# A decoder layer on one core: lead-in steps begin with the rounded x, VectorE rounds x's second half, convolution operations move to rounds 8 to 10

## The chip, the cores and the metric

The kernel runs on one core of one Trainium2 chip. Its time is the device time of one execution in microseconds (us). The engines are TensorE (PE, with its weight loads as PEld), VectorE (DVE), ScalarE (ACT), GpSimd (POOL) and SyncE (SP), which here only issues transfers. Line numbers are those of the kernel before unless said otherwise.

## The reference

One decoder layer over x (1024 tokens of 1024 features, float32), cut to what matters:

```python
shift, scale, gate = jnp.split(silu(c) @ w_ada + b_ada, 3, axis=-1)
h = _rms_norm(x, norm_w) * (1.0 + scale) + shift
q, k, v, gate_a, u, gate_b = jnp.split(h @ w_in, splits, axis=-1)
q, k = rope(rms_norm(q)), rope(rms_norm(k))
y_a = sliding_window_sink_attention(q, k, v, sinks) * silu(gate_a)
y_b = conformer_conv(u, ...) * silu(gate_b)   # GLU, 31 causal taps, LayerNorm, SiLU
x = x + gate * (jnp.concatenate([y_a, y_b], -1) @ w_out)
```

## The kernel before

**Products of matrices.** Each float32 factor is split into a part rounded to float32r ("hi") and the rest ("lo"). A product is three matmuls: hi by hi, lo weight by hi x, hi weight by lo x. `channel_step` issues these three for one 128-row block k of the 1024 features; eight blocks make a channel tile (128 output channels by 512 tokens). `h[:, 0]` holds the rounded modulated x, `h[:, 1]` its rest.

**The lead-in.** x is transposed by TensorE (`x_transposes(idx)`, idx 0 to 7 for the first 512 tokens, 8 to 15 for the second) into the two banks of `tr`. ScalarE's `modulate(idx)` reads a bank twice: it writes the modulated x unrounded (`h32`, two buffers) and then rounded (`h[:, 0]`), and then counts `a_h32`. VectorE's `split_h(idx)` subtracts the two (`h[:, 1]`) and counts `d_hlo`. For the modulation of block k a column of adaLN is needed: VectorE sums it (`ada_sums`, slabs of `w_ada` by eight transfers' worth of rows), TensorE adds it over the partitions (`ada_cols(k)`), ScalarE turns it into `modA`, `modB` (`factors`). In lead-in step k TensorE runs block k of four channel tiles at once (`early`), after waiting for `d_hlo`. `keep_busy` issues matmuls whose result is not used.

**After the lead-in.** Channel tile 4 runs from the first 512 tokens; tile 5 does too, with the transposes of x's second half between its steps; tile 6 is the first that reads the second half, and waits at each block for `d_hlo`. Tiles 7 to 15 follow. ScalarE and VectorE make the GLU from them (`tanh_g`, `glu`), which frees the banks. VectorE also adds up the gate columns (`gate_sum(0..7)`, each from a 512 KB transfer into the ring `raw` of three buffers, which the weights share: a buffer is loaded again when its sum counts `d_gp`).

**The convolution** is 200 VectorE operations in a fixed list (`conv_order`); `conv(n)` issues the next n. They stand between other work of VectorE: 62 before the rounds, the rest in the rounds.

**The rounds** n = 0 to 15. In round n TensorE projects Q, K, V of token block n (n under 8, `L777` to `L779`) or a gate channel tile, and between the steps runs attention: `transpose_qk` and `scores` of block n - 2, `transpose_p` and `times_v` of block n - 4. VectorE in its round n does the RoPE of block n - 1, `previous_keys` and `row_max` of block n - 2, `denominators` of n - 3, gates (`gate`, from n = 8) and convolution operations. The order on each engine is the order of the code; engines meet only through semaphores.

**LayerNorm of the convolution.** After the last operation VectorE adds the four channel blocks (`channel_sum`), TensorE adds over the partitions (`ln_mean`, L796, then `ln_var`, L804), VectorE copies the variance out, GpSimd makes the reciprocal deviations (L517), and `ln_scale` (L812) spreads that row over the partitions into `ps`; `normed` and `swish` of VectorE wait for it.

The lines at the places named:

```python
for dst in (h32[:, idx % 2, :], h[:, 0, k, half * HALF:(half + 1) * HALF]):   # L955, ScalarE
pe.wait_ge(d_hlo, k + 1)                                                     # L601, lead-in step
gate_sum(0); gate_sum(1); gate_sum(2)                                        # L1290, VectorE
if (m, half, k) == (6, 1, 6): ln_scale()                                     # L829, TensorE
```

## Time and profile before

| | us |
|---|---|
| median of 3 runs (430.77 to 432.27) | 431.35 |
| the profiled execution, its own time | 431.71 |
| its span | 430.0 |
| PE busy | 408.4 (95%) |
| DVE busy | 334.0 (78%) |
| ACT busy | 217.5 (51%) |
| POOL busy | 110.0 (26%) |

The span runs from the first to the last instruction; 1.71 us of the execution lie around it. Matmuls are pipelined and their ends modelled, so PE's busy time says when it had work, not that it ran at its peak. An idle time in brackets behind a row names what ended it.

### The profile page before, as it was taken

To read this page: it belongs to the slowest core of one execution; us is meant where nothing else is said; L and a number is where in the kernel's file an instruction comes from. 1 tells how busy PE (TensorE), PEld (TensorE's weight loads), DVE (VectorE), ACT (ScalarE), POOL (GpSimd) and SP (SyncE) were. 2 spreads that over 40 slices of the span, in tenths; PEclk is the share of its full clock that TensorE was granted. 3 is DMA by queue.
4 is the path that set the end of the run, shared out by engine and by line. 5 is a ranking of instruction groups with operands and counts; after the bars stand their busy time and mean duration, and the time that the engine had idled before them with its cause. 6 is when DMAs were issued, how large, how long until landed. Compare 5 with 4: busy or idle time off the path is not lost.

```text
span 430.0 us, 5914 instructions
## 1 busy us (share of the span) xinstructions
PE 408.4 (95%) x2102; PEld 327.6 (76%) x2102; DVE 334.0 (78%) x554; ACT 217.5 (51%) x496; POOL 110.0 (26%) x150
## 2 busy tenths in 40 slices
PE   0899998999999998999999999999999999999996
PEld 0577785888888887778776767777788888888886
DVE  2789777599999999999989797799995996222222
ACT  3768777025211137887788989524166784100000
POOL 1400050002420443354225316973031005100000
PEclk9999998999999999999999999999999999999999
DMA  7999656306930000004003466993637059951111
GB/s 274 353 316 351 243 178 207 99 0 167 231 61 2 6 8 7 7 2 155 0 8 91 75 124 124 166 103 71 125 74 124 2 195 252 259 125 49 50 49 50
DMA packets 54327, 51.40 MB, mean 120 GB/s; under 512 B 19271, under 2 KB 49275, under 8 KB 54298
## 3 DMA queue, kind: packets, MB, share of 16 engines
q1 hardware_dynamic: 38256, 41.50, 31.0%
q0 software_dynamic: 15904, 9.44, 16.8%
q8 instruction: 17, 0.28, 0.3%
q10 hardware_dynamic: 138, 0.09, 0.1%
q14 instruction: 12, 0.10, 0.1%
HBM read 46.82 MB, written 4.19 MB: 119 GB/s over the span
## 4 chain that ended last, share of the span: by engine, by line
PE 54%; DVE 28%; issue 3%; ACT 2%; DMA 1%; POOL 1%; DVEq 0%; ACTq 0%
PE pm L573 7%; PE pm L574 6%; PE pm L575 6%; DVE cacc L1326 4%; PE pm L846 4%; PE pm L845 4%; PE pm L847 4%; DVE cacc L1346 3%; DVE z L1333 3%; PE tr L846 3%; PE tr L845 3%; PE tr L847 3%; PE ps L702 2%; DVE cacc L1333 2%; DVE z L1346 2%
## 5 line engine op out<-in xcount | busy, mean ns | idle before, releaser
L573 PE MATMUL pm<-h,wts 128*128 128x512 f32 x224 | 90.4, 404 | 1.3 <-DVE gb L1461 0.8
L574 PE MATMUL pm<-h,wts 128*128 128x512 f32 x224 | 87.6, 391 | 0.0
L575 PE MATMUL pm<-h,wts 128*128 128x512 f32 x224 | 87.4, 390 | 0.0
L573 PEld LDWEIGHTS pm<-h,wts 128*128 128x128 f32 x224 | 42.2, 188 | 13.4 <-issue 2.4
L575 PEld LDWEIGHTS pm<-h,wts 128*128 128x128 f32 x224 | 42.2, 188 | 9.1
L574 PEld LDWEIGHTS pm<-h,wts 128*128 128x128 f32 x224 | 42.3, 189 | 8.2 <-issue 0.2
L921 ACT ACTIVATE wts<-raw 128x1024 fp32r<-128x1024 f32 x30 | 31.2, 1051 | 33.4 <-PE pm L575 17.4
L777 PE MATMUL pm<-wts,h 128*128 128x256 f32 (+1 forms) x128 | 45.1, 352 | 0.1
L778 PE MATMUL pm<-wts,h 128*128 128x256 f32 (+1 forms) x128 | 43.1, 337 | 0.0
L779 PE MATMUL pm<-wts,h 128*128 128x256 f32 (+1 forms) x128 | 43.1, 337 | 0.0
L440 POOL DMA_DIRECT2D wts<-in_w_in x22 | 28.8, 2697 | 51.6 <-ACT wts L923 51.6
L1333 DVE SCALAR_TENSOR_TENSOR z<-z,cw 128x513 f32<-128x513 f32 x42 | 31.7, 754 | 3.8 <-POOL pcur L483 3.6
L1053 ACT ACTIVATE sel<-sel,nmx,rsq 128x128 f32<-128x128 f32 x64 | 30.7, 482 | 2.2 <-DVE sdiff L1445 2.0
L440 POOL DMA_DIRECT2D wts<-in_w_out x12 | 13.4, 1275 | 68.0 <-ACT wts L923 68.0
L777 PEld LDWEIGHTS pm<-wts,h 128*128 128x128 f32 x128 | 24.2, 189 | 6.7 <-issue 3.5
L845 PE MATMUL pm<-wts,h 128*128 128x512 f32 x72 | 28.0, 389 | 0.0
L846 PE MATMUL pm<-wts,h 128*128 128x512 f32 x72 | 28.0, 389 | 0.0
L847 PE MATMUL pm<-wts,h 128*128 128x512 f32 x72 | 28.0, 389 | 0.0
L1617 DVE TENSOR_TENSOR obuf<-pm,gbc 128x512 f32<-128x512 f32 x9 | 6.2, 692 | 27.4 <-PE pm L847 27.4
L956 ACT ACTIVATE h<-tr,modB,modA 128x512 f32<-128x512 f32 (+1 forms) x32 | 22.8, 777 | 7.0 <-PE tr L537 4.8
L779 PEld LDWEIGHTS pm<-wts,h 128*128 128x128 f32 x128 | 24.2, 189 | 2.7
L778 PEld LDWEIGHTS pm<-wts,h 128*128 128x128 f32 x128 | 24.3, 190 | 2.3
(209 smaller groups left out, 901.7 us busy)
## 6 DMA issues: line engine op xcount, KB each, us to landing
slab<-in_w_ada SPq DMA_DIRECT2D x16, 512.0 KB, 8.2
raw<-in_w_in SPq DMA_DIRECT2D x14, 512.0 KB, 4.9
xs<-in_x SPq DMA_DIRECT2D x8, 512.0 KB, 8.8
raw<-in_w_ada SPq DMA_DIRECT2D x8, 512.0 KB, 4.5
xr<-in_x SPq DMA_DIRECT2D x8, 512.0 KB, 5.9
out<-xr SPq DMA_DIRECT2D x15, 256.0 KB, 2.7
wts<-in_w_in POOLq DMA_DIRECT2D x6, 512.0 KB, 9.5
raw<-in_w_in SPq DMA_DIRECT2D x8, 256.0 KB, 8.0
```

The source lines that it names most:

```text
L440: gp.dma_start(to, src, accum_op=ALU.add).then_inc(g_add[ADDED.index(i)], 16)
L573: pe.matmul(out, hi_w, hi_x, start=first, stop=False)
L574: pe.matmul(out, lo_w, hi_x, start=False, stop=False)
L575: return pe.matmul(out, hi_w, lo_x, start=False, stop=last)
L777: pe.matmul(o, x_hi, w_hi, start=(k == 0), stop=False)
L778: pe.matmul(o, x_hi, w_lo, start=False, stop=False)
L779: last = pe.matmul(o, x_lo, w_hi, start=False, stop=(k == KT - 1))
L845: pe.matmul(o, h[:, 0, k, ts], w[0], start=(k == 0), stop=False)
L846: pe.matmul(o, h[:, 0, k, ts], w[1], start=False, stop=False)
L847: return pe.matmul(o, h[:, 1, k, ts], w[0], start=False, stop=(k == KT - 1))
L921: act.activation(whalf(i, 0), src, ACT.Copy).then_inc(a_hi, 1)
L1333: ins = dve.scalar_tensor_tensor(out=tmp, in0=src, scalar=weight, in1=tmp, op0=ALU.mult, op1=ALU.add)
```

## The change

- `a_hr` is a new semaphore. In the first half of x, ScalarE writes the rounded x first and counts `a_hr`, then writes `h32` and counts `a_h32`.
- A lead-in step waits for `a_hr` and runs the eight matmuls that read the rounded x (both weight parts, four tiles), then waits for `d_hlo` and runs the four that read the rest. `ada_cols(k + 1)` stands between the second and the third tile of the eight. The four `keep_busy` matmuls of step 2 are gone; of those after `ada_cols(1)`, one and a half banks stand before the transposes and none behind them (before: two and one and a half).
- Channel tile 4 has its 16 matmuls with the rounded weights first, waiting for ScalarE's `a_hi`; the 8 with the weights' rest follow after `wait_split`.
- In the second half of x ScalarE writes `h32` alone; VectorE copies it to `h[:, 0]`, waits for that copy, and subtracts.
- VectorE's order: `gate_sum(0)`, the eight split steps, the first two `glu`, then `gate_sum(1)` to `(7)` (before: sums 0 to 2, split steps with sums 3 to 5 between, sums 6 and 7, and the two `glu` later).
- Convolution operations: 18 become 16 before the rounds; in round 0 11 become 5, in round 1 4 become 3, in round 9 9 become 8, in round 10 9 become 12, in round 11 12 become 11; rounds 8 and 9 get 4 more each behind `row_max`. The list and its length of 200 stay.
- `ln_scale` is issued three steps sooner, in front of step 3 of tile (6, 1) and not of step 6.

```diff
             keep_busy(pm[:, 2, :], 2)
             ada_cols(1)
-            keep_busy(pm[:, 2, :], 2)
+            keep_busy(pm[:, 2, :], 1)
+            keep_busy(pm[:, 2, 0:256], 1)
             x_transposes(0)
             x_transposes(1)
-            keep_busy(pm[:, 2, :], 1)
-            keep_busy(pm[:, 2, 0:256], 1)
...
                 if 0 < k < KT - 1:
                     x_transposes(k + 1)
-                    if k == 2:
-                        pe.wait_ge(a_ab, 4)
-                        keep_busy(ps[:, 1, 256:512], 4)
-                    if k > 1:
-                        ada_cols(k + 1)
-                pe.wait_ge(d_hlo, k + 1)
+                pe.wait_ge(a_hr, k + 1)
                 if k % 2 == 0:
                     pe.wait_ge(d_wlo, k // 2 + 1)
                 for e, (bank, slot, col) in enumerate(early):
-                    if (k, e) == (1, 3):
-                        ada_cols(2)
-                    last = channel_step(bank, slot, col, 0, k)
+                    if e == 2 and 0 < k < KT - 1:
+                        ada_cols(k + 1)
+                    for part in range(2):
+                        pe.matmul(bank, wts[:, slot + 1, part, k, col:col + P], h[:, 0, k, 0:HALF],
+                                  start=(k == 0 and part == 0), stop=False)
+                pe.wait_ge(d_hlo, k + 1)
+                for bank, slot, col in early:
+                    last = pe.matmul(bank, wts[:, slot + 1, 0, k, col:col + P], h[:, 1, k, 0:HALF],
+                                     start=False, stop=(k == KT - 1))
...
             pe.wait_ge(a_ab, 16)
+            pe.wait_ge(a_hi, 6)
+            for k in range(KT):
+                for part in range(2):
+                    pe.matmul(ps[:, 1, :], wts[:, 3, 0, k, 0:P], h[:, part, k, 0:HALF], start=(k == 0 and part == 0), stop=False)
             wait_split(pe, 2)
-            channel_tile(4, ps[:, 1, :], 2, 0, 0)
+            for k in range(KT):
+                last = pe.matmul(ps[:, 1, :], wts[:, 3, 1, k, 0:P], h[:, 0, k, 0:HALF], start=False, stop=(k == KT - 1))
+            last.then_inc(p_main, 1)
...
-                        if (m, half, k) == (6, 1, 6):
+                        if (m, half, k) == (6, 1, 3):
                             ln_scale()
...
-                for dst in (h32[:, idx % 2, :], h[:, 0, k, half * HALF:(half + 1) * HALF]):
-                    last = act.activation(dst, tr[:, idx % 2, :], ACT.Identity, scale=modA[:, k:k + 1],
-                                          bias=modB[:, k:k + 1])
-                last.then_inc(a_h32, 1)
+                if idx < KT:
+                    act.activation(h[:, 0, k, half * HALF:(half + 1) * HALF], tr[:, idx % 2, :], ACT.Identity,
+                                   scale=modA[:, k:k + 1], bias=modB[:, k:k + 1]).then_inc(a_hr, 1)
+                act.activation(h32[:, idx % 2, :], tr[:, idx % 2, :], ACT.Identity, scale=modA[:, k:k + 1],
+                               bias=modB[:, k:k + 1]).then_inc(a_h32, 1)
...
                 dve.wait_ge(a_h32, idx + 1)
+                if idx >= KT:
+                    link(dve.tensor_copy(h[:, 0, k, sl], h32[:, idx % 2, :]))
...
-            gate_sum(0)
-            gate_sum(1)
-            gate_sum(2)
-            for idx in range(KT, 2 * KT):
-                split_h(idx)
-                if idx < KT + 3:
-                    gate_sum(idx - KT + 3)
-            gate_sum(6)
-            gate_sum(7)
...
+            gate_sum(0)
+            for idx in range(KT, 2 * KT):
+                split_h(idx)
+            glu(0, 0, pm[:, 2, :], 2, 1)
+            glu(1, 0, ps[:, 0, :], 3, 2)
+            for i in range(1, KT):
+                gate_sum(i)
...
                 if n == 0:
-                    conv(11)
+                    conv(5)
```

The order of VectorE's instructions behind the normalised x of the second half (`xs`), before; `h<-h_64,h` is the subtraction, `gacc` a gate sum, `z` the GLU, `h_64` the buffers `h32`:

```order
L1223 TENSOR_SCALAR xs<-xs,rsx 128x1024 x4
L1283 TENSOR_SCALAR gacc<-raw,cact 128x1024
L1286 SCALAR_TENSOR_TENSOR gacc<-raw,cact,gacc 128x1024 x2
L1246 TENSOR_TENSOR h<-h_64,h 128x512
L1286 SCALAR_TENSOR_TENSOR gacc<-raw,cact,gacc 128x1024
...
L1246 TENSOR_TENSOR h<-h_64,h 128x512 x5
L1286 SCALAR_TENSOR_TENSOR gacc<-raw,cact,gacc 128x1024 x2
```

And the same place now (its line numbers are those of the changed kernel); the pair of `CAST` and subtraction stands there eight times:

```order
L1230 TENSOR_SCALAR xs<-xs,rsx 128x1024 x4
L1292 TENSOR_SCALAR gacc<-raw,cact 128x1024
L1254 CAST h<-h_64 128x512
L1255 TENSOR_TENSOR h<-h_64,h 128x512
...
L1303 SCALAR_TENSOR_TENSOR z<-z,pm 128x2x256
L1303 SCALAR_TENSOR_TENSOR z<-z,ps 128x2x256
L1295 SCALAR_TENSOR_TENSOR gacc<-raw,cact,gacc 128x1024 x7
```

Seven gate sums moved behind the last split step and the first two GLU operations; eight copies came in.

TensorE in lead-in step 2, before: the transposes of block 3 (`tr`), the unused matmuls, the adaLN column, then twelve matmuls in threes per tile:

```order
L537 MATMUL tr<-ident,xs 128x128 x4
L546 MATMUL ps<-ones 128x256 x4
L567 MATMUL ps<-ones,ada_acc 128x1 x2
L573 MATMUL pm<-h,wts 128x512
L574 MATMUL pm<-h,wts 128x512
L575 MATMUL pm<-h,wts 128x512
```

And now, where L602 reads the rounded x and L606 the rest:

```order
L537 MATMUL tr<-ident,xs 128x128 x4
L602 MATMUL pm<-h,wts 128x512 x4
L567 MATMUL ps<-ones,ada_acc 128x1 x2
L602 MATMUL pm<-h,wts 128x512 x2
L602 MATMUL ps<-h,wts 128x512 x2
L606 MATMUL pm<-h,wts 128x512 x3
L606 MATMUL ps<-h,wts 128x512
```

The adaLN column moved behind four matmuls that do not need it, and the matmuls with x's rest moved to the step's end.

VectorE at the end of round 8, before: the row maxima of block 6 (`nmx`), then the gates of rounds 8 and 9:

```order
L1439 TENSOR_REDUCE nmx<-sel_51 128x8
L1442 TENSOR_TENSOR nmx<-nmx,rsq 128x8
L1444 TENSOR_TENSOR nmx<-nmx,nsnk 128x8
L1445 TENSOR_TENSOR sdiff<-nmx,snk 128x8
L1461 SCALAR_TENSOR_TENSOR gb<-gb,pm 128x512 x2
```

And now:

```order
L1444 TENSOR_REDUCE nmx<-sel_51 128x8
L1447 TENSOR_TENSOR nmx<-nmx,rsq 128x8
L1449 TENSOR_TENSOR nmx<-nmx,nsnk 128x8
L1450 TENSOR_TENSOR sdiff<-nmx,snk 128x8
L1333 SCALAR_TENSOR_TENSOR z<-z,cw 128x512
L1353 SCALAR_TENSOR_TENSOR cacc<-z,cws,cacc 128x512
L1343 SCALAR_TENSOR_TENSOR z<-z,cols 128x512
L1349 TENSOR_TENSOR z<-z 128x527
L1466 SCALAR_TENSOR_TENSOR gb<-gb,pm 128x512 x2
```

Four convolution operations moved in front of the two gates.

## Rows read from the trace of the kernel before

**Rows 1.** The page, part 1: busy us (share of the span) x instructions.

```profile
PE 408.4 (95%) x2102; PEld 327.6 (76%) x2102; DVE 334.0 (78%) x554; ACT 217.5 (51%) x496; POOL 110.0 (26%) x150
```

**Rows 2.** Timeline, PE, lead-in: start, duration, instructions merged [idle before <- what ended it].

```profile
17.05 2.74 PE L546 MATMUL pm<-ones 128*128 128x512 f32 x4
19.63 1.04 PE L537 MATMUL tr<-ident,xs 128*128 128x128 f32 x8
...
22.50 0.50 PE L573 MATMUL pm<-h,wts 128*128 128x512 f32 x1 [0.54 <-DVE h L1246]
...
30.03 1.89 PE L546 MATMUL ps<-ones 128*128 128x256 f32 x8
...
47.53 0.58 PE L567 MATMUL ps<-ones,ada_acc 128*128 128x1 f32 x4 [0.39 <-DVE ada_acc L1239]
...
53.85 0.39 PE L573 MATMUL ps<-h,wts 128*128 128x512 f32 x1
```

**Rows 3.** Timeline, ACT and DVE, lead-in.

```profile
20.27 1.45 ACT L956 ACTIVATE h<-tr,modB,modA 128x512 f32<-128x512 f32 x2 [1.94 <-PE tr L537]
...
23.88 0.69 DVE L1246 TENSOR_TENSOR h<-h,h 128x512 fp32r<-128x512 f32 x1 [0.65 <-ACT h L956]
...
31.05 0.69 DVE L1246 TENSOR_TENSOR h<-h,h 128x512 fp32r<-128x512 f32 x1 [0.46 <-ACT h L956]
...
44.47 2.46 DVE L1235 SCALAR_TENSOR_TENSOR ada_acc<-slab,cact,ada_acc 128x256 f32<-128x256 f32 x6
```

**Rows 4.** Timeline, PE, tiles 5 (`pv`), 6 and 7 (`pm`).

```profile
69.56 0.90 PE L537 MATMUL tr<-ident,xs 128*128 128x128 f32 x4 [1.34 <-ACT h L956]
...
72.25 0.78 PE L573 MATMUL pm<-h,wts 128*128 128x512 f32 x1
...
78.26 0.39 PE L573 MATMUL pm<-h,wts 128*128 128x512 f32 x1
78.94 0.39 PE L573 MATMUL pm<-h,wts 128*128 128x512 f32 x1
```

**Rows 5.** Windows: stretch, then busy us of PE, PEld, DVE, ACT, POOL; granted clock.

```profile
71.00:72.00 1.00, 1.00 (x5) 0.60 (x5) 0.66 (x1) 1.00 (x3) 0.00 (x0) 0.50 0.77 259
...
240.00:260.00 20.00, 20.00 (x112) 15.17 (x111) 17.78 (x30) 18.45 (x45) 5.82 (x8) 1.00 0.63 113
260.00:280.00 20.00, 20.00 (x113) 14.92 (x112) 14.65 (x26) 15.08 (x42) 18.42 (x24) 1.00 1.00 154
```

**Rows 6.** Timeline, DVE, gate sums to the first convolution operations.

```profile
58.38 0.75 DVE L1223 TENSOR_SCALAR xs<-xs,rsx 128x1024 f32<-128x1024 f32 x1 [0.71 <-POOL rsx L434]
...
74.72 2.67 DVE L1286 SCALAR_TENSOR_TENSOR gacc<-raw,cact,gacc 128x1024 f32<-128x1024 f32 x2
...
84.70 0.49 DVE L1323 TENSOR_SCALAR cacc<-z,cw 128x512 f32<-128x512 f32 x1
...
97.43 2.35 DVE L1252 TENSOR_TENSOR wts<-raw,wts 128x1024 fp32r<-128x1024 f32 x2
```

**Rows 7.** The page, part 6: KB each, median us from issue to landing.

```profile
raw<-in_w_ada SPq DMA_DIRECT2D x8, 512.0 KB, 4.5
```

**Rows 8.** Timeline, DVE and PE, weights' rest of unit K0 and round 3.

```profile
130.27 2.35 DVE L1252 TENSOR_TENSOR wts<-raw,wts 128x1024 fp32r<-128x1024 f32 x2
...
134.51 0.28 PE L777 MATMUL pm<-wts,h 128*128 128x256 f32 x1
...
166.67 1.13 PE L702 MATMUL ps<-kT,qT 64*128 64x256 f32 x8 [1.58 <-DVE sel L1427]
```

**Rows 9.** Timeline, DVE, PE and POOL, row of means to row of deviations.

```profile
306.64 1.23 DVE L1476 TENSOR_TENSOR lnA<-lnA,z 128x1024 f32<-128x1024 f32 x1
...
307.92 1.98 PE L796 MATMUL ps<-lnA,ones 128*128 128x512 f32 x4
...
321.44 1.67 POOL L517 TENSOR_TENSOR rsx<-tiny,mhalf 128x8 f32<-128x8 f32 x1
...
325.10 1.95 PE L812 MATMUL ps<-ident,rsx 128*128 128x128 f32 x16
```

More of the change, by code:

```diff
@@ L1307, in glu @@
                                          op0=ALU.add, op1=ALU.mult).then_inc(d_glu, 1)
+            gate_sum(0)
[5 more added lines that the diff above has]
+                gate_sum(i)
+            dve.memset(z[:, :, :].rearrange("p c (b m) -> p c b m", b=2)[:, :, :, 0:PAD // 2], 0.0).then_inc(d_link, 1)
+            linked[0] += 1
             done = [0]
@@ L1357, in _ @@
             pads = linked[0]
-            glu(0, 0, pm[:, 2, :], 2, 1)
-            glu(1, 0, ps[:, 0, :], 3, 2)
             glu(0, 1, pm[:, 1, :], 7, 5)
@@ L1365, in _ @@
             glu(1, 1, ps[:, 0, :], 9, 6)
-            conv(18)
+            conv(16)
             glu(2, 0, pm[:, 2, :], 12, 3)
@@ L1517, in _ @@
                 if n == 9:
-                    conv(9)
+                    conv(8)
                 if n == 10:
@@ L1526, in _ @@
                 if n == 10:
-                    conv(9)
+                    conv(12)
                 if n == 11:
-                    conv(12)
+                    conv(11)
                     channel_sum(1)
@@ L1543, in _ @@
                     row_max(b2)
-                if n == 1:
-                    conv(4)
+                if n in (1, 8, 9):
+                    conv({1: 3, 8: 4, 9: 4}[n])
                 if 8 <= n < 15 and n != 10:
```

4 lines of the change are left out of this document (1 added, 3 removed).

## The prediction

> **What bounds the kernel now.** I read the page's part 1 first: PE is busy for 408.4 of 430.0 us, DVE for 334.0 [rows 1]. So the time can fall only where PE idles, runs at its lower clock, or issues matmuls that nobody needs; those 21.6 idle us had to be found by the timeline of PE. It shows four places. Before 22.50 PE waits for the first modulated x. In the lead-in it waits 0.39 for a column of adaLN in step 6, and step 2 carries four unused matmuls, from 30.03 to 31.76 [rows 2]. In the second half of x it waits for ScalarE, the longest 1.34, and then works at clock 0.50, the lower of its two levels (1.2 GHz and not 2.4) [rows 4, 5]. In round 3 it waits 1.58 for VectorE [rows 8]. The chain of waits adds the second fact: from 84 to 184 us it runs on VectorE almost alone, through the convolution. PE hardly idles there, so the two engines are level. A gain of PE in the lead-in is kept only if VectorE comes sooner by as much; otherwise it turns into new waits of PE.
>
> **1. The first half of x.** PE's steps. The transposes start at 19.63, behind two unused banks of which the first runs at the low clock; half a bank fewer stands there now. VectorE's x is ready just then, so I put the start at 19.2. ScalarE took the first bank 0.64 after the start of the transposes, and its two writes last 1.45 together, 0.75 each [rows 2, 3]. With the rounded x first, PE can start 0.64 + 0.75 + 0.1 behind 19.2, at 20.7, where it started at 22.50: 1.8 sooner.
>
> What follows is set by VectorE. Its work in a lead-in step is the split (0.60 to the next start), six sums (2.46) and the last add (0.35): 3.4, and 4.6 where it also makes the weights' rest (1.15); PE's own is 12 matmuls x 0.227, the transposes 0.43, the column 0.36: 3.5. From 31.05 to 47 VectorE has no pause, so the lead-in moves by what its pauses give before that: 0.65 at 23.88 and 0.46 at 31.05, both waits for ScalarE's second write [rows 3]. ScalarE's first step is 0.5 sooner, and its step 2 follows a column that PE now reaches 2.3 sooner; of the 1.11 I take 0.95. So the last column is ready at 46.4 where it was at 47.35. Then PE: column until 46.75, eight matmuls of step 6 until 48.6, while ScalarE makes the factors and the last rounded x (0.6 + 0.75, ready at 48.25), step 7 with 12 matmuls until 51.35. Tile 4 began at 53.85 [rows 2]: **2.5 sooner**. More than VectorE's 0.95, since behind the last column nothing waits for the unrounded x and its split any longer, and two thirds of a step are left to fill the time. The four unused matmuls cost nothing then and give nothing now: VectorE's pace hides them. PE has new pauses instead, at the columns: by the same sums 1.0, 0.5, 1.1 and 0.95 us. Tile 4's new order is free: ScalarE's last weights are there at 50.8, VectorE's rest at 52.2, and 16 matmuls run from 51.35 to 55.0.
>
> **2. The second half.** Before, tile 4 starts at 53.85 and tile 6 ends at 78.26, 24.4 us [rows 2, 4]. PE's own work there is 3 tiles x 8 blocks x 0.68 (row 78.94 less row 78.26) and eight transposes x 0.44: 19.85. So 4.55 are waits and low clock. After: x's last block is normalised at 59.05, behind ScalarE's squares [rows 6], which start 1.2 sooner: 57.9, where PE would want it at 57.5; 0.35 of waiting stays. Then ScalarE has one write of 0.75 per block, not two, and no gate sum (1.28) stands between VectorE's splits. VectorE's block is a copy and a subtraction. The copy is in no row; the nearest above is the subtraction, 0.69 with the same output, the nearest below a tensor_scalar of 512 elements, 0.49 [rows 3, 6]. I take the lower, since it also has one source; the pair then is 0.45 + 0.05 + 0.65, about 1.2, and 1.5 by the upper end. Eight pairs from 59.4 end at 69.0 (71.4 by the upper end). PE wants the last at 71.0, so even the upper end costs 0.4. Tile 6 ends at 71.7: **4.05 sooner, 6.55 in all**.
>
> On such a copy the Trainium skill ("VectorE: DVE Perf Modes", section "Mode 2×_2P — use both read ports for one tensor") says that an op with one tensor from SBUF reads it through both ports and gives two results a cycle even in float32, which an op with two tensors cannot. By that rule the sum is the one above, by 0.69 it is 0.4 less of a gain; the two rows agree with the rule, but no row here shows it for an output in float32r.
>
> **3. What VectorE owes for it.** The gate sums 1 to 7 now stand behind the splits and two glu (69.0 + 1.2 = 70.2). Three find their data in the ring. The fourth is issued when sum 1 frees its buffer (71.5), and a transfer lands after 4.5, 3.5 at best [rows 7]; with 1.28 per sum (2.67 for two [rows 6]) the four late ones end at 76.9, 78.2, 79.7 and 81.7 (81.0 at best, 83.5 if each waits its 4.5). The convolution starts at 82.6 (81.9 to 84.4), before at 84.70: **2.1 sooner**, not 6.5. From here the due times, VectorE against PE:
> - 20 operations take 12.7 (84.70 to 97.43), 0.66 each [rows 6]. The weights' rest for tile 12 is ready at 97.6; PE, 6.5 sooner, wants it at 99. Free.
> - 18 to 16 operations give 1.3 more. K0's first rest was ready at 131.4 and is at 128.0; PE wanted it at 134.51 and wants it at 128.0 [rows 8]. I price 0.1; each us that the convolution starts later than 82.6 costs a us here.
> - Round 0 loses six operations (4.0) and round 1 one (0.66): VectorE is 3.4 + 4.65 = 8.1 sooner from round 2.
> - Round 3: PE comes 6.5 sooner, VectorE 8.1, so the 1.58 shrinks to nothing and PE is 8.0 sooner. From round 4 the chain of waits was PE's and stays PE's.
> - The operations taken out (2 + 6 + 1) come back: 4 in round 8, 4 - 1 in round 9, 3 in round 10, less 1 in round 11, nine net, up to ten ahead at once, 6.6 us. VectorE's idle time there was 2.22 + 5.35 = 7.57 [rows 5]. They fit if they fall where it waited; not all will. Row maxima and probabilities of the last blocks may come up to 1 us late, and I charge 0.5.
>
> **4. The deviations' row.** PE issues it at 325.10, and GpSimd had it ready at 323.11. Three steps sooner is 3 x 0.68: 323.06 [rows 9]. So PE waits 0.05 and a semaphore's time, 0.2 by my estimate, and the normed blocks start 1.8 sooner. PE never waited for those, so I book **0.2 lost**. Bounds: 0 to 1.
>
> **The sum**: -6.55 + 0.1 - 1.5 (round 3) + 0.5 + 0.2 = -7.25, rounded up to -7.5 for small waits of PE in rounds 5 to 12 which an earlier VectorE ends. The profiled execution took 431.71, 0.36 over the median of 431.35. From it 424.2, from the median 423.85; I say **424.0**.
>
> **Rivals.**
> *A. VectorE keeps the middle.* If nine operations in rounds 8 to 11 find no idle time (ScalarE's tanh waits in turn for VectorE), VectorE reaches the row of means only by its earlier start. There both are level: its last sum ends at 307.87, PE's row starts at 307.92 [rows 9]. Gain then 2.1 plus about half of 2.6: 428.5. For: the chain; against: 7.57 us idle.
> *B. The clock falls in the lead-in.* Before, it fell after the pause of 1.34, and cost half of the some 3.8 us spent at 0.50 [rows 4, 5]. The new pauses at the columns are up to 1.1. Each fall costs up to 1.9, of which VectorE's pace hides a part: with two, 426.8. Before, PE was without a pause of 0.4 in these steps thanks also to the four unused matmuls. The Trainium skill ("TensorE: Matmul & The Clock Gate", section "What's actually happening") speaks against the change here: the clock is set by how busy TensorE has been of late, so taking away unused work can lower it. By that rule the time would be this rival's; the rows show one fall after long pauses and none after 0.39 or 0.54.
> *C. More.* If rounds 8 to 11 cost nothing and small waits go: 422.0.
> *D. Slower: the splits hold everything.* If copy, subtraction and ScalarE's write run one after another (0.75 + 0.69 + 0.61 and three semaphore times of 0.1: 2.35 per block), eight blocks from 59.4 end at 78.2, and the convolution starts at 89.3, 4.6 later than before; K0's rest then holds PE by 1.2 beyond its old time, and with VectorE's waits in rounds 8 to 11 only half filled the row of means comes 2.5 later: 434. It decides from 84.70 on: a convolution that starts later loses. Against: two `h32` buffers and two banks let the write run beside the split.
> *E. The change does not do what it says.* If the adaLN transfers, and not VectorE, pace the lead-in and PE's transposes pace the second half, nothing moves before 70 us: 430.8.
>
> **Chances.** Forecast 0.56 (422.6 to 425.8), A 0.14, B 0.13, C 0.07, D 0.06, E 0.04. The range from 422.0 to 428.8 holds the forecast, B and the better part of A and C. What this measurement tells from no change is 0.3%, 1.3 us. Faster: forecast, A, B, C, 0.90; the same: E, 0.04; slower: D, 0.06.
>
> **What would show it.** In the changed profile: PE's first projection matmul at 20.7; tile 4 at 51.4; the `CAST` at 0.49 or below, and the last subtraction near 69; tile 6 ending at 71.7 with granted clock 1.00 from 65 to 75; the gate sums ending near 81.7, with two waits for `raw`; the first convolution operation at 82.6; no wait above 0.5 at K0's weights; no wait of PE for `sel` in round 3; VectorE's idle time from 232 to 272 under 2.5; the row of means at 300; the row of deviations 0.2 late. I am wrong if the convolution starts after 84.7, if the clock in the lead-in is under 1.00, or if PE waits for VectorE before the row of means by more than 1 us.

## The result, and the profile after

The changed kernel takes 427.74 us (median of 5 executions, 427.46 to 428.81); the kernel before, measured beside it, 431.80 (430.77 to 432.27). The ratio is 0.9916 (95% interval 0.9898 to 0.9934): 3.6 us faster by the ratio, 4.06 by the medians. 424.0 us were forecast, 7.4 sooner than the 431.35 from which the forecast started. So the direction was right and half of the gain was missing. The same two kernels measured once more, further below, gave 0.9910 (0.9897 to 0.9922).

The profiled execution of the changed kernel has a span of 426.2 us against 430.0. The page's part 1, which answers to [rows 1]:

```profile
PE 402.5 (94%) x2090; PEld 323.7 (76%) x2090; DVE 337.7 (79%) x562; ACT 212.4 (50%) x488; POOL 113.4 (27%) x150
```

VectorE has eight operations more and ScalarE eight fewer, the copies; TensorE has 12 matmuls fewer.

**The lead-in.** Timeline of PE; the columns are start, duration, instruction, and in brackets the idle time before it and what ended it. It answers to [rows 2].

```profile
21.22 1.66 PE L602 MATMUL pm<-h,wts 128*128 128x512 f32 x6 [0.43 <-ACT h L962]
...
47.38 0.58 PE L567 MATMUL ps<-ones,ada_acc 128*128 128x1 f32 x4 [0.94 <-DVE ada_acc L1246]
...
52.48 0.84 PE L627 MATMUL ps<-h,wts 128*128 128x512 f32 x3
```

The first projection matmul comes 1.3 us sooner, the new pauses at the columns are there (0.94 before the last), and tile 4 starts at 52.48 where it was at 53.85. In twelve further traces that share this lead-in and keep the clock, tile 4 starts between 51.59 and 52.22; this execution is 0.3 to 0.9 later than they are.

**The second half and the gate sums.** Timeline of VectorE (`L1254` is the copy, `L1255` the subtraction, `L1295` the gate sums), which answers to [rows 6]:

```profile
68.67 0.43 DVE L1254 CAST h<-h 128x512 fp32r<-128x512 f32 x1
69.13 0.69 DVE L1255 TENSOR_TENSOR h<-h,h 128x512 fp32r<-128x512 f32 x1
...
75.75 1.29 DVE L1295 SCALAR_TENSOR_TENSOR gacc<-raw,cact,gacc 128x1024 f32<-128x1024 f32 x1 [0.74 <-DMA raw<-in_w_ada]
78.08 1.28 DVE L1295 SCALAR_TENSOR_TENSOR gacc<-raw,cact,gacc 128x1024 f32<-128x1024 f32 x1 [1.04 <-DMA raw<-in_w_ada]
80.11 2.67 DVE L1295 SCALAR_TENSOR_TENSOR gacc<-raw,cact,gacc 128x1024 f32<-128x1024 f32 x2 [0.75 <-DMA raw<-in_w_ada]
...
83.98 0.49 DVE L1330 TENSOR_SCALAR cacc<-z,cw 128x512 f32<-128x512 f32 x1
```

The copy is 0.43 us and the last subtraction starts at 69.13, as forecast. TensorE has no low clock here any more, and tile 7 starts at 73.12 where it started at 78.26 [rows 4]:

```profile
73.12 0.39 PE L573 MATMUL pm<-h,wts 128*128 128x512 f32 x1
```

```profile
65.00:75.00 10.00, 10.00 (x52) 8.38 (x51) 9.64 (x14) 3.67 (x6) 0.00 (x0) 1.00 0.16 47
```

That row is a window: stretch, its length, busy time of PE, PEld, DVE, ACT, POOL, granted clock. So 5.1 us of the lead are in hand. But three gate sums wait for their rows, 2.5 us together, and the convolution starts only 0.7 sooner. What holds its start has changed: before, VectorE had its gate sums done and stood still for TensorE's tile 7 right in front of it,

```profile
83.90 0.69 DVE L1306 SCALAR_TENSOR_TENSOR z<-z,pm 128x512 f32<-128x512 f32 x1 [4.83 <-PE pm L575]
```

and now the gate sums themselves end at 82.78, after tile 7.

**The stretch in which it was decided.** I cut both traces at two events: VectorE's first convolution operation, and TensorE's row of means, which follows VectorE's last channel sum. One window of the kernel before:

```profile
84.70:307.92 223.22, 219.90 (x1220) 174.64 (x1218) 211.03 (x352) 125.73 (x346) 86.13 (x112) 1.00 0.40 74
```

and of the changed kernel, with the two windows that answer to [rows 5]:

```profile
83.98:304.03 220.05, 215.41 (x1201) 171.03 (x1199) 211.06 (x352) 125.78 (x346) 88.95 (x112) 1.00 0.41 78
240.00:260.00 20.00, 18.98 (x104) 13.90 (x104) 19.14 (x32) 18.06 (x54) 8.61 (x13) 1.00 0.67 129
260.00:280.00 20.00, 17.84 (x98) 12.93 (x95) 17.16 (x29) 11.51 (x28) 19.86 (x22) 1.00 0.98 124
```

The reader should look at the DVE column: 352 operations and 211.0 us in both. The stretch is VectorE's load plus its pauses: 211.03 + 12.19 before, 211.06 + 8.99 after. The gain at the row of means is therefore 0.72 (start of the convolution) + 3.20 (pauses) - 0.03 = 3.89, and from there to the end of the span the two take 122.0 and 122.2. Such a sum could be written for any engine. That VectorE is the right one shows at the stretch's end: the row of means starts 0.06 us behind VectorE's last sum,

```profile
302.75 1.22 DVE L1481 TENSOR_TENSOR lnA<-lnA,z 128x1024 f32<-128x1024 f32 x1
304.03 1.98 PE L802 MATMUL ps<-lnA,ones 128*128 128x512 f32 x4
```

and 0.05 to 0.09 behind it in all 17 traces of this case, although the row lies anywhere from 300.02 to 308.15. So nothing that TensorE gains in between counts by itself. The waits of VectorE in this stretch (us in total, times, longest), before:

```profile
DVE gb L1461 <- ACT gb L1103: 3.9, 5, 1.4
DVE z L1333 <- POOL pcur L483: 3.6, 2, 2.9
DVE wts L1252 <- ACT wts L921: 1.1, 1, 1.1
```

and after:

```profile
DVE z L1353 <- POOL pcur L483: 3.4, 2, 2.8
DVE wts L1261 <- ACT wts L927: 1.1, 1, 1.1
DVE nmx L1444 <- POOL sel L504: 1.0, 1, 1.0
```

The waits at the gates, 3.9 us, are filled by the moved operations. The waits for GpSimd's masks of the probabilities (`pcur`) are not: 3.6 before, 3.4 after. One for GpSimd's part of the scores (`sel`) is new; it ends at 151.89, long before rounds 8 to 11. `L1353` waits by the kernel's own code: in rounds 10 and 11 VectorE stops for `g_mask` before more convolution operations.

**The masks.** GpSimd's timeline, blocks 6 and 7, before (each mask is L477, L481, L483):

```profile
261.24 0.63 POOL L477 TENSOR_SCALAR_AFFINE_SELECT pprev<-pcur 128x512 f32<-128x512 f32 x1 [12.06 <-ACT pcur L1035]
...
274.52 0.63 POOL L477 TENSOR_SCALAR_AFFINE_SELECT pprev<-pcur 128x512 f32<-128x512 f32 x1
```

and after:

```profile
255.36 1.08 POOL L477 TENSOR_SCALAR_AFFINE_SELECT pprev<-pcur 128x512 f32<-128x512 f32 x1 [11.18 <-ACT pcur L1042]
...
269.45 2.88 POOL L477 TENSOR_SCALAR_AFFINE_SELECT pprev<-pcur 128x512 f32<-128x512 f32 x1
```

The same instruction takes 2.88 where it took 0.63. It starts at 269.45, 5.07 sooner than before, beside the ninth of VectorE's run of twelve operations, and ends at 272.33, 0.5 behind that run's last:

```profile
271.09 0.74 DVE L1340 SCALAR_TENSOR_TENSOR z<-z,cw 128x513 f32<-128x513 f32 x1
274.64 0.75 DVE L1353 SCALAR_TENSOR_TENSOR z<-z,cws 128x512 f32<-128x512 f32 x1 [2.81 <-POOL pcur L483]
```

**The deviations' row.** GpSimd has the deviations ready at 319.22, and TensorE's row follows at 319.27, where it stood 2.0 us behind them before [rows 9]; VectorE's wait for the row fell from 3.8 to 2.0:

```profile
317.55 1.67 POOL L517 TENSOR_TENSOR rsx<-tiny,mhalf 128x8 f32<-128x8 f32 x1
```

### The profile page after: what moved, and what is told of

Read it like the earlier page. It is cut to its first block, busy times and chain, and to the rows that moved or that the text cites. A ratio compares the mean times of both kernels' runs of the same rounds, so it can differ in the third digit from the quotient of the medians.

```text
span 426.2 us, 5891 instructions
## 1 busy us (share of the span) xinstructions
PE 402.5 (94%) x2090; PEld 323.7 (76%) x2090; DVE 337.7 (79%) x562; ACT 212.4 (50%) x488; POOL 113.4 (27%) x150
## 4 chain that ended last, share of the span: by engine, by line
PE 52%; DVE 23%; POOL 6%; ACT 3%; issue 3%; DMA 1%; DVEq 0%; ACTq 0%; POOLq 0%
PE pm L783 4%; PE pm L573 4%; PE pm L784 4%; PE pm L785 4%; PE pm L575 4%; PE pm L574 4%; PE pm L852 4%; PE pm L851 4%; PE pm L853 4%; DVE cacc L1333 3%; PE tr L852 3%; PE tr L851 3%; PE tr L853 3%; POOL wts L440 2%; PE ps L708 2%
## 5 line engine op out<-in xcount | busy, mean ns | idle before, releaser
L573 PE MATMUL pm<-h,wts 128*128 128x512 f32 x200 | 79.8, 399 | 0.8 <-DVE gb L1466 0.8
L575 PE MATMUL pm<-h,wts 128*128 128x512 f32 x200 | 77.9, 390 | 0.0
L574 PE MATMUL pm<-h,wts 128*128 128x512 f32 x200 | 77.9, 390 | 0.0
L573 PEld LDWEIGHTS pm<-h,wts 128*128 128x128 f32 x200 | 37.5, 188 | 11.1 <-issue 2.4
L575 PEld LDWEIGHTS pm<-h,wts 128*128 128x128 f32 x200 | 37.5, 188 | 8.0
L574 PEld LDWEIGHTS pm<-h,wts 128*128 128x128 f32 x200 | 37.6, 188 | 7.5 <-issue 0.2
L1353 DVE SCALAR_TENSOR_TENSOR z<-z,cws 128x512 f32<-128x512 f32 x30 | 22.4, 748 | 3.8 <-POOL pcur L483 3.4
```

The lines of the kernel that those rows point to most:

```text
L573: pe.matmul(out, hi_w, hi_x, start=first, stop=False)
L574: pe.matmul(out, lo_w, hi_x, start=False, stop=False)
L575: return pe.matmul(out, hi_w, lo_x, start=False, stop=last)
```

## The experiments

Theory T1: GpSimd's masks are held up while VectorE's convolution operations run without a gap, and that is what the moved operations cost. Theory T5: VectorE's load and its pauses set the row of means. The rivals stand in the expectations. All ratios are against the kernel before, measured beside each kernel (its median there was 431.25 to 431.80); so ratios compare better than medians. "Stretch" is first convolution operation to row of means, as above, in one profiled execution of each kernel. "Small masks" leaves out most of the last three blocks' masks and does not compute the layer.

| kernel | convolution starts | stretch | row of means | median us | ratio (95% interval) |
|---|---|---|---|---|---|
| before | 84.70 | 223.2 | 307.92 | 431.80 | 1 |
| changed | 83.98 | 220.05 | 304.03 | 427.74 | 0.9916 (0.9898 to 0.9934) |
| counts back | 82.71 | 223.2 | 305.92 | 430.61 | 0.9985 (0.9972 to 0.9997) |
| counts alone | 84.05 | 224.1 | 308.15 | 431.92 | 1.0021 (1.0006 to 1.0036) |
| lead-in alone | 83.71 | 223.3 | 307.02 | 430.57 | 0.9980 (0.9966 to 0.9994) |
| ScalarE writes both | 85.18 | 220.4 | 305.55 | 429.59 | 0.9959 (0.9943 to 0.9974) |
| fewer at round 10 | 82.76 | 220.9 | 303.63 | 428.01 | 0.9934 (0.9914 to 0.9954) |
| no stop for the masks | 83.55 | 224.2 | 307.71 | 431.77 | 1.0001 (0.9986 to 1.0016) |
| small masks | 82.91 | 217.1 | 300.02 | 424.60 | 0.9842 (0.9826 to 0.9858) |

**1. The counts back.** One of the six counts:

```diff
                 if n == 0:
-                    conv(5)
+                    conv(11)
```

> The changed kernel with the convolution's operations spread over the rounds as in the kernel before (18 for 16 ahead of the rounds, 11 for 5 in round 0, 4 for 3 in round 1, 9 and nothing extra in rounds 8 and 9, then 9 and 12); everything else of the change stays. Theory T1 (contention: GpSimd's masks are slowed by VectorE operations put beside them in rounds 8 to 10): with fewer operations beside them the masks of blocks 5 and 6 need 0.63, 0.42 and 0.41 us each again and the L477 of block 7 falls from 2.88 us to about 0.63; but eight operations more (8 x 0.67 = 5.3 us) stand ahead of round 0, where the convolution starts only 0.7 us sooner than before, so that the first matrix product of the rounds waits on VectorE again and the rounds start 4 to 5 us later than in the changed kernel: 429.5 to 431 us. Rival R3 (the second half and lead-in gain is simply lost later, whatever VectorE does): 427.7 us, as the changed kernel.

Measured 430.61 us: T1's range. L477 is 0.63 again in blocks 6 and 7 (0.62 in the trace of block 6):

```profile
259.20 0.62 POOL L477 TENSOR_SCALAR_AFFINE_SELECT pprev<-pcur 128x512 f32<-128x512 f32 x1 [12.06 <-ACT pcur L1042]
...
272.50 0.63 POOL L477 TENSOR_SCALAR_AFFINE_SELECT pprev<-pcur 128x512 f32<-128x512 f32 x1
```

The rest of the change without the counts shortens nothing behind 82.71: the stretch is 223.2, to 0.01 that of before. But the range does not speak for T1 alone. The first product of the rounds waits 3.0 us for VectorE, as the expectation also said, and TensorE's clock is 0.58 from 142 to 146 behind it. And VectorE waits for the masks as long as before the change, though nothing holds them up:

```profile
DVE z L1340 <- POOL pcur L483: 3.6, 2, 2.9
```

So the masks' waits are there without any hold-up, and the second half of T1, that the hold-up is what the moved operations cost, is not shown.

**2. Fewer at round 10.**

```diff
-                    conv(12)
+                    conv(8)
...
-                    conv(11)
+                    conv(15)
```

> The changed kernel with 8 instead of 12 operations of the convolution in round 10 and 15 instead of 11 in round 11, after the masks of block 7; all else as changed. T1 (contention): VectorE's run of back-to-back operations ends at 269.1 instead of 271.8 us, L477 of block 7 (starts 269.45) takes 0.6 to 0.9 us instead of 2.88, the masks end at 271 to 271.5 instead of 274.56, VectorE waits for them about 2 us and the PV product of block 7 does not wait 1.39 us; four more operations then stand ahead of the first channel sum: it starts 0.5 to 1.0 us sooner (286.41 before the edit), total 426.7 to 427.2 us. Rival R2 (GpSimd is slow there by itself, as the tail of its eight DMA issues of 10.35 us that come just before): L477 keeps 2.9 us, the masks end at 274.6, and the four operations come on top: first channel sum 2.7 us later, 430 us.

```profile
268.25 1.03 POOL L477 TENSOR_SCALAR_AFFINE_SELECT pprev<-pcur 128x512 f32<-128x512 f32 x1
```

L477 falls to 1.03 and with it R2 (GpSimd is slow there by itself), since the eight DMA issues of 10.35 us stand in front of it as before. But no time came of it (428.01): the stretch is 0.8 longer, where I expected 0.5 to 1.0 less. VectorE now waits 3.59 for the masks instead of 2.81, and the four operations still have to be done. T1's mechanism held, my price of it did not: VectorE's twelve operations were useful work, and what counts is how long it stands still for the masks. With four of them behind the masks these end at 271.56 and not at 274.61, and nothing is gained by it.

**3. The counts alone**: the kernel before, with the six edits of the first experiment the other way, as

```diff
                 if n == 10:
-                    conv(9)
+                    conv(12)
```

> The kernel before with the change's counts of convolution operations alone (16, 5, 3, 8, 12, 11 and 4 more in rounds 8 and 9), nothing else of the change. The rounds start 2.5 to 3 us sooner, as the waits of TensorE for VectorE at the first product of the rounds (1.58 us) and round 3 go; T1: in rounds 8 to 11 the masks cost 2.5 to 3 us more as in the changed kernel, so that 0 to 1.5 us of it are left: 430 to 431.8 us. Rival R3 (the loss in rounds 8 to 11 comes with the earlier second half, not with the operations moved there): the full 2.5 to 3 us stay, 428.5 to 429.2 us.

431.92 us, 0.2% slower than before and 0.1 us above T1's range. The masks of block 7 are held up just as much (2.88), so it is the counts and not the earlier start that do it. L477 shows how the lead goes: it starts 2.1 us sooner than before in block 5, 1.8 in block 6, 0.95 in block 7, and the row of means comes 0.2 later. VectorE, now early, waits for TensorE's products instead:

```profile
DVE ssq L1386 <- ACT v L1029: 3.6, 2, 3.3
DVE z L1346 <- POOL pcur L483: 3.3, 2, 2.8
```

Together with experiment 1: neither the counts nor the rest of the change shortens the stretch (+0.9 and 0.0), both together do by 3.2. By the ratios the counts alone lose 0.9 us, the rest alone gains 0.6, both together gain 3.6.

**4. The second gate sum ahead of the splits.**

```diff
             gate_sum(0)
+            gate_sum(1)
             for idx in range(KT, 2 * KT):
```

> The changed kernel with the second gate sum in front of the eight splits of the second half, not behind them (as before three stood there). Theory T4: the gate sums are bound by the landing of their rows (waits of 0.74, 1.04 and 0.75 us behind the splits), since each sum frees the buffer for a later load; with one more in front, a load starts 6 us sooner and one of the three waits goes, the convolution starts 0.7 us sooner, the splits start 0.7 us later but have waits for the transposes of x to take that: 427.0 to 427.7 us. Rival: the loads are slow by themselves and all waits stay, and the second half's products start 0.7 us later: 427.7 to 428.4 us.

426.86 us, ratio 0.9903 (0.9889 to 0.9917), a little under both ranges. The convolution starts at 81.53, but the waits for rows are still 0.69, 1.34 and 0.50, as long as before the edit. The stretch grows to 220.7. See 12.

**5. No stop for the masks.**

```diff
                 if n == 11:
-                    dve.wait_ge(g_mask, 2 * NT)
                     conv(5)
```

> The changed kernel without VectorE's wait for the masks of block 7 in round 11 (it stood ahead of five operations of the convolution and one gate, and took 2.81 us in the trace of the changed kernel). T1 (VectorE's operations hold up GpSimd's masks as long as they run without a gap): VectorE goes on, L477 of block 7 (starts 269.45) and the five masks behind it take until VectorE comes to its next gap or wait, so they end at 276 to 278 instead of 274.56 us; TensorE's PV product of block 7 waits 3 to 5 us instead of 1.39; VectorE's first channel sum comes up to 2.8 us sooner; in all 427 to 429 us. Rival R2 (the 2.88 us are GpSimd's own): masks still end at 274.6, VectorE gains its 2.81 us, 425.2 us.

```profile
268.82 6.21 POOL L477 TENSOR_SCALAR_AFFINE_SELECT pprev<-pcur 128x512 f32<-128x512 f32 x1
275.10 0.41 POOL L481 TENSOR_SCALAR_AFFINE_SELECT pcur<-pcur 128x256 f32<-128x256 f32 x1
```

```profile
273.78 0.75 DVE L1333 SCALAR_TENSOR_TENSOR z<-z,cw 128x512 f32<-128x512 f32 x1
```

```profile
277.36 1.12 PE L739 MATMUL pv<-pcur,vmix 128*64 128x256 f32 x4 [4.73 <-POOL pcur L483]
```

This is the clearest showing of T1. An instruction that takes 0.63 takes 6.21 and ends 0.5 behind VectorE's last operation; the next one, with VectorE still, takes its 0.41. Rival R2 falls. The total (431.77, all of the change's gain lost) was worse than I wrote: VectorE's first channel sum comes 3.7 us later and not sooner, since VectorE then waits 7.11 us for ScalarE's part of a gate, and TensorE's clock is 0.56 in a stretch that holds its own wait:

```profile
274.00:280.00 6.00, 2.64 (x16) 1.07 (x16) 0.53 (x1) 0.00 (x0) 5.86 (x10) 0.56 0.20 26
```

**6. The third gate sum ahead, too.**

```diff
             gate_sum(0)
+            gate_sum(1)
+            gate_sum(2)
             for idx in range(KT, 2 * KT):
```

> As the experiment with the second gate sum ahead of the splits, with the third there too. T4 (a gate sum behind the splits is bound by its row's landing, each early sum starts one load sooner): VectorE waits for no row behind the splits or for one, the convolution starts another 0.7 us sooner, the splits start 0.7 us later: 426 to 427 us. Rival: two sums ahead already use up the slack ahead of the splits, the second half of the products of x starts 0.7 us later and the rounds with it: 427 to 427.7 us.

427.5 us. The convolution starts at 81.38, no sooner than with two sums (0.7 was expected), and tile 6 starts 0.9 later; the stretch is 222.0, with 1.7 us of new waits of VectorE for TensorE's products. The rival was right.

**7. ScalarE writes both** (no copy on VectorE).

```diff
-                if idx < KT:
+                if True:
                     act.activation(h[:, 0, k, half * HALF:(half + 1) * HALF], ...)
...
-                if idx >= KT:
-                    link(dve.tensor_copy(h[:, 0, k, sl], h32[:, idx % 2, :]))
```

> The changed kernel with ScalarE writing both h and h32 in the second half again, VectorE not copying. Theory (ScalarE's two ACTIVATEs of a step set the pace of the second half before, and the copy took that away): the eight steps are 0.3 to 0.5 us longer each, tile 7 starts 3 to 4 us later (near 76.5 us) and VectorE's splits end as much later, but it saves VectorE 8 x 0.43 = 3.4 us; the rounds start 0.5 to 3 us later: 428.5 to 430 us. Rival (VectorE's total is what counts up to the rounds): unchanged or sooner, 426.5 to 427.7 us.

429.59 us, within the theory's range. VectorE's subtractions then wait 0.65 each for ScalarE, every 1.34 us instead of 1.13, and tile 6 starts at 68.35 against 66.6 to 67.6. In the kernel with the lead-in alone, which has the gate sums between the splits as well, it starts at 71.71. So of the second half's gain the copy brings 1 to 2 us and the gate sums' new place about 3 (3.4, less the 0.5 by which that kernel's tile 4 starts later).

**8. The lead-in alone**: the kernel before, with the change's `modulate` order for all 16 steps and TensorE's part up to tile 4.

```diff
-                for dst in (h32[:, idx % 2, :], h[:, 0, k, half * HALF:(half + 1) * HALF]):
+                if True:
+                    act.activation(h[:, 0, k, half * HALF:(half + 1) * HALF], ...).then_inc(a_hr, 1)
+                act.activation(h32[:, idx % 2, :], ...).then_inc(a_h32, 1)
```

> The kernel before with the lead-in part alone (in all sixteen steps ScalarE writes the rounded x first, TensorE's products of the rounded x come ahead of those of the rest, the extra products that keep TensorE busy in step 2 are gone, tile 4 in the order of the change). By the trace of the changed kernel the first half ends 2.0 us sooner, net of the start; the second half is still ScalarE's pace: it starts 2 us sooner and all of it stays up to the gate sums, where rows that land late take 0.5 to 1 us back: 429.8 to 430.6 us. Rival (the lead-in's gain ends at the gate sums' rows): 431.2 us, as before.

430.57 us: 0.2% faster, as expected. Tile 4 starts at 52.22, the convolution at 83.71.

**9. Small masks.**

```diff
+                if b >= 5:
+                    gp.affine_select(out=pprev[g][0:64, :, 0:8], in_=pcur[g][0:64, :, 0:8], ...)
+                    gp.affine_select(out=pcur[g][0:64, :, 0:8], in_=pcur[g][0:64, :, 0:8], ...)
+                    return
```

> The changed kernel with GpSimd's masks of blocks 5, 6 and 7 cut to a corner of 64 x 8 elements a head in two operations instead of three full ones (the rest of these masks is left out, so the attention of the last blocks is not the reference's). Theory T5 (from conv start to the mean row VectorE is the bound: 211.0 us of work plus its waits, 9.0 us, of which 3.4 are for these masks): both waits for the masks nearly go (0.5 to 1 us left), TensorE's 0.83 and 1.39 us before the PV products go, the row of the means comes 2.4 to 3 us sooner, 424.8 to 425.5 us. Rival T6 (TensorE is the bound in rounds 9 to 11, VectorE's waits are slack): it gains at most TensorE's 2.2 us of waits or less, 426 us or more.

The masks are cut to a corner here and the result is not the layer's; the run only prices them. 424.60 us, 3.1 below the changed kernel's median, slightly more than expected. The stretch falls from 220.05 to 217.11:

```profile
82.91:300.02 217.11, 215.28 (x1201) 171.05 (x1200) 209.83 (x352) 125.87 (x346) 83.09 (x106) 1.00 0.42 80
```

VectorE's same 352 operations are 1.2 us shorter, its pauses 1.7. T5 holds and T6 falls. What the run prices is all of the masks' work, the waits for them and VectorE's slower operations beside them, and not the hold-up alone. Even a mask of 64 x 32 elements is held:

```profile
267.27 1.75 POOL L477 TENSOR_SCALAR_AFFINE_SELECT pprev<-pcur 64x32 f32<-64x32 f32 x1 [1.10 <-ACT pcur L1050]
269.09 0.23 POOL L481 TENSOR_SCALAR_AFFINE_SELECT pcur<-pcur 64x32 f32<-64x32 f32 x1
```

**10. The unused matmuls back in step 2.**

```diff
+                    if k == 2:
+                        pe.wait_ge(a_ab, 4)
+                        keep_busy(ps[:, 1, 256:512], 4)
                 pe.wait_ge(a_hr, k + 1)
```

> The changed kernel with the four extra products of step 2 (256 columns each) that keep TensorE busy in the lead-in. The granted clock is 1.00 in the lead-in without them, so they only cost their own time where TensorE does not wait, 4 x 0.11 to 0.2 us: 427.7 to 428.3 us. Rival (the clock is only just held without them, so that some executions lose it): median 427.4 us or less.

```profile
29.68 1.89 PE L546 MATMUL ps<-ones 128*128 128x256 f32 x8
31.22 1.28 PE L605 MATMUL pm<-h,wts 128*128 128x512 f32 x4
```

428.75 us, ratio 0.9937 (0.9924 to 0.9949), 1.0 above the changed kernel: they take 1.54 of TensorE's time, tile 4 starts at 53.36, the convolution at 84.74. That is above both expectations; the lead-in is TensorE's at that point and nothing hides them. The six executions lie within 0.5 us (428.43 to 428.90), those of the changed kernel within 3.0.

**11. The deviations' row back; small operations in the waits.**

```diff
-                        if (m, half, k) == (6, 1, 3):
+                        if (m, half, k) == (6, 1, 6):
                             ln_scale()
```

> The changed kernel with the deviations' row back at step 6 of that product, from step 3. The end after the mean row was as long before and after (122.1 us each from the mean row to the end of the span), although VectorE's wait for the row fell from 3.8 to 2.0 us. Theory (that wait is slack): 427.7 us, within 0.2. Rival (it carried 0.5 us or more, hidden by another loss): 428.2 to 429 us.

427.08 us, ratio 0.9904 (0.9888 to 0.9919), below both ranges, but the intervals of the two kernels overlap. The traces are sharper. The row of means to the end of the span takes 121.98 to 122.04 us in the five traces that have the row at step 6 (this one, the kernel before, the counts alone, the lead-in alone and the last kernel of experiment 12), and 122.22 to 122.27 in the twelve that have it at step 3. The sooner row costs 0.2 us, although VectorE's wait for it is 1.8 shorter.

```diff
             gate_sum(0)
             gate_sum(1)
...
-            for i in range(2, KT):
+            for i in range(2, 5):
                 gate_sum(i)
+            (the memset of z's padding, lnc, cws)
+            for i in range(5, KT):
+                gate_sum(i)
```

> The experiment with the second gate sum ahead of the splits (426.86 us), and VectorE's memset of the padding and its small operations on the columns (0.16, 0.32 and 0.21 us) moved from behind the gate sums to behind the fifth, where VectorE waits for a row. Theory T5 (each us by which VectorE's convolution starts sooner comes off the end, since VectorE is the bound up to the mean row): the convolution starts 0.4 us sooner, 426.4 to 426.6 us. Rival T6 (TensorE bounds): 426.9 us, no change against it.

427.12 us, ratio 0.9901 (0.9884 to 0.9917): a miss. The convolution starts at 81.46, against 81.53 without the edit: the operations did fit into the waits, but the row behind them was not there sooner. T5 in its strict form ("each us at the convolution's start comes off the end") was not tested by it, and the stretches of 220.7 to 222.0 at starts of 81.3 to 81.7 speak against it: there VectorE waits 0.3 to 1.7 us for TensorE's products, and at starts from 83.16 to 86.07 it does not.

**12. Three kernels side by side**: the changed kernel again, the second gate sum ahead, and that with the deviations' row back.

> The changed kernel itself, as the measure for the two others of this comparison: 427.5 to 428 us.

> The second gate sum ahead of the splits, in one comparison with the changed kernel. Theory T4 (late rows at the gate sums are a part of the shortfall): 0.6 to 1.2 us below the changed kernel's median. Rival (the difference of 0.9 us lay between the two comparisons): within 0.3 us of it.

> The second gate sum ahead of the splits, and the deviations' row back at step 6. Theory (VectorE's wait for that row is slack for the end): within 0.3 us of the run beside it that has the gate sum alone. Rival 1 (TensorE's earlier row splits the product and costs, as the forecast charged it): 0.2 to 0.6 us below it. Rival 2 (the wait is on the path): 0.5 us or more above it.

427.74, 427.88 and 426.58 us; ratios 0.9910 (0.9897 to 0.9922), 0.9915 (0.9898 to 0.9932) and 0.9889 (0.9877 to 0.9902). So the second gate sum alone shows no gain that can be told, against T4 and against its own first figure. The third kernel has the lowest median of all that leave nothing out, 1.2 below the changed kernel's, but its interval touches the changed kernel's; whether it is faster stays open. Of the 1.3 us against the kernel beside it the traces show only the 0.3 behind the row of means (121.98 against 122.27), and its row of means came later, not sooner (302.84 and 302.47, spans 424.8 and 424.7).

The profiled execution of the changed kernel in this comparison (429.97 us) shows something else. Its clock falls in the lead-in, behind the pause at the last column:

```profile
48.63 0.58 PE L567 MATMUL ps<-ones,ada_acc 128*128 128x1 f32 x4 [0.95 <-DVE ada_acc L1246]
...
55.31 3.79 PE L627 MATMUL ps<-h,wts 128*128 128x512 f32 x16
```

```profile
50.00:53.00 3.00, 3.00 (x9) 2.37 (x8) 1.44 (x2) 3.00 (x4) 0.00 (x0) 0.55 0.14 53
```

Tile 4 starts 2.8 us later than in the other trace of this kernel, the convolution at 86.07, 2.1 later, and the row of means 1.95 later. Not all of it is the clock's: the first projection matmul was 0.5 later already (21.75), and the last column 1.25 later (48.63 against 47.38), both at clock 1.00. The stretch at the lower clock adds the other 1.6. The stretch from convolution to row of means is 219.91. Of the eleven executions of the changed kernel this is the only one whose mean clock is 0.996; the others have 1.0 (of the kernel before, two of the eleven executions beside it have 0.996).

## Why the prediction was half right

**Step 1, the lead-in: right in the main.** Forecast were the first matmul at 20.7 and tile 4 at 51.35. Measured are 20.9 to 21.8 and 51.6 to 52.5 (the changed kernel's own trace, 52.48, is the latest that keeps the clock; against the 53.85 of before that is 1.4 sooner, where 2.5 was forecast). One sentence in it was wrong: "The four unused matmuls cost nothing". In the new order they cost 0.9 to 1.8 us at tile 4 (53.36, against 52.48 in the changed kernel's own trace and 51.6 in the earliest) and 1.0 at the end (experiment 10), so part of the gain put down to the order of the writes is theirs.

**Step 2, the second half: right.** The copy at 0.43 against 0.45, the last subtraction at 69.13 against 69, the clock at 1.00; tile 6 ends at 73.12 against 71.7, and 0.8 of these 1.4 us are the later tile 4 of this trace (tile 6 starts at 67.57 here, at 66.73 where tile 4 starts at 51.60). On the copy, the Trainium skill's rule ("VectorE: DVE Perf Modes", section "Mode 2×_2P — use both read ports for one tensor") agrees with the row: 0.43 for the copy, 0.69 for the subtraction of the same size with its two tensors, and this for an output in float32r too.

**Step 3, the convolution's start: 1.4 us too soon for this trace, within 1 us for others.** 82.6 was forecast; 83.98 came, and 82.71 to 83.55 in five traces that differ behind this point only. Three sums waited for rows, not two.

**Step 3, rounds 8 to 11: here it failed.** "VectorE's idle time there was 2.22 + 5.35 = 7.57. They fit if they fall where it waited ... I charge 0.5." The nine operations need 6.6 us of idle time. They filled 3.9: from 240 to 280 us VectorE is idle for 3.70, where it was for 7.57. What they filled are the waits at the gates (3.9 before). The other half, 3.6 us, were waits for GpSimd's masks behind a stop in the code, and 3.4 are left. Operations put in front of that stop delay the masks, operations put behind it leave the wait as it is. So 2.7 us of the moved work found no room, and 0.5 was charged. The forecast's own sign, idle time from 232 to 272 under 2.5, came true (1.2), but only since the long mask wait lies just behind it, from 271.8 to 274.6.

The forecast had the row of means at 300, so a stretch of 217.4 from its start of the convolution; the stretch is 220.05. With most of the masks cut away (experiment 9) it is 217.11. That this is so near to 217.4 is in part luck: 1.2 us of it are VectorE's own operations becoming shorter, and the pauses are 7.3 where the forecast needs 6.4. Together 4.0 us are missing at the row of means, of which 1.4 are the later start and 2.65 the stretch. These two account for the shortfall in this trace; over the executions the stretch is the steady part, since it was 219.9 to 220.1 in four traces with starts from 83.16 to 86.07.

Behind it is a wrong picture of what bounds. The sum followed TensorE: 6.55, round 3, and so on. The middle of the rounds did come 6.25 us sooner than before (a row maximum at 206.11 against 212.37), and gave 2.4 back by the row of means, since the end is set by VectorE's 211.0 us, its start and its pauses. That was readable before: the window from 84.70 to 307.92 has it in one row. Rival A ("VectorE keeps the middle", 428.5, chance 0.14) was the nearest in time, 0.8 off. That is mostly luck: it let the row of means gain by the earlier start alone, 2.1, where the start gave 0.7 and the pauses 3.2, and its reason, ScalarE's tanh, is the wait that was filled.

The Trainium skill has a rule that bears on this ("SBUF — State Buffer", section "Who interferes with whom"): a VectorE instruction with two inputs in SBUF contends with a GpSimd instruction that reads SBUF, and the pair of ports that the two share is an exclusive lock. The traces agree that GpSimd is held, with 0.63 grown to 2.88 and 6.21; the prediction did not weigh it. In the traces it is held over many instructions of VectorE in a row, not one. That it is the shared port, and not something else of the two engines, no run here shows; other kinds of VectorE operations beside the masks were not tried.

**Round 3: right in kind, too large.** The wait of 1.58 before the same product [rows 8] shrank to 0.69 and not to nothing:

```profile
160.43 1.14 PE L708 MATMUL ps<-kT,qT 64*128 64x256 f32 x8 [0.69 <-DVE sel L1432]
```

So the lead grew there from 5.35 to 6.24, by 0.9 and not 1.5.

**Step 4, the deviations' row: right.** 0.2 was booked, and 0.2 is what the five traces without the move and the twelve with it differ by (experiment 11).

**Rival B, the clock in the lead-in: false for the median, true in one execution of eleven**, at the place named, behind the pause at a column. The low clock cost 1.6 us there at tile 4 (up to 1.9 was the forecast's price of a fall); the execution is 2.0 longer than the other profiled one. That the other nine kept the clock is read from their mean clock of 1.0; their pauses were not traced.

## What to carry over

Look for the engine whose busy time plus pauses makes up a long stretch between two events, and write the gain as start plus pauses of that engine; sooner work of any other engine counts only where it ends one of these pauses. Before idle time is counted as room for moved work, ask for each piece what ended it: a wait for another engine's result that the moved work itself delays is no room. Two parts of a change can be worth next to nothing each (0.6 gained, 0.9 lost) and 3.6 us together, when one brings an engine's input sooner and the other gives it the time to use it.

## What the runs showed of the hardware

A GpSimd select that reads and writes SBUF can be held for as long as VectorE issues `SCALAR_TENSOR_TENSOR` operations back to back: 0.63 us alone, 2.88 and 6.21 beside such runs, each time until 0.5 us after the run's last operation; a select of 64 x 32 elements, 0.23 alone, took 1.75 and ended 0.1 after it. TensorE's product that reads the masks waited 4.73 us beside the longest one. It is not always the loser: at 255.36 it got in after 1.08, and VectorE's operation beside it took 1.12 instead of 0.74. I had also not expected that TensorE, with the same code, holds its clock through a pause of 0.94 us in one execution and drops to the lower level behind one of 0.95 in another. In the second a pause of 0.35 for ScalarE stood 2 us ahead of it, which the first does not have; whether that makes the difference no run here shows.
